# Spreading eight gate rows over the partitions: four transposes of a repeated column in place of one fp32 product with a diagonal

## The reference, cut to what matters

```python
mod = c_act @ w_ada[l] + b_ada[l]
sh1, sc1, g1, sh2, sc2, g2, sh3, sc3, g3 = jnp.split(mod, N_MOD, axis=-1)
x = x + 0.5 * g1[:, None, :] * swiglu(modulate(x, sh1, sc1), ffn1_gate[l], ffn1_up[l], ffn1_down[l])
x = x + g2[:, None, :] * token_mix(modulate(x, sh2, sc2), ...)
x = x + 0.5 * g3[:, None, :] * swiglu(modulate(x, sh3, sc3), ffn2_gate[l], ffn2_up[l], ffn2_down[l])
# hybrid layer: x + gate1 * (merged @ w_o), then x + gate2 * moe, without the 0.5
```

## Time and profile before

| | |
|---|---|
| Three timed runs | 1815.82, 1820.74, 1822.90 us, median 1820.74 |
| The profiled execution's own time | 1816.8 us |
| Its span, first to last instruction | 1815.0 us |
| PE busy | 1741.0 us, 96% |
| DVE busy | 1379.6 us, 76% |
| ACT busy | 967.7 us, 53% |
| DMA | 437.43 MB, 241 GB/s over the span |
| Mean granted clock of PE | 0.988 |
| L1032, diagonals on DVE | 64 instructions, 281 ns each in the middle of the list |
| L1892, products with diagonals on PE | 32 records, 592 ns each |

### The profile page before, as it was taken

One profiled execution on the slowest core, in us unless ns is written; L12 is line 12 of the kernel. 1 busy time (PEld: TensorE's weight loads), 2 busy tenths in 40 slices (PEclk: granted clock), 3 DMA queues, 4 the chain that ended last, 5 costly groups with the idle time before them and its releaser, 6 DMA issues.

```text
span 1815.0 us, 24952 instructions
## 1 busy us (share of the span) xinstructions
PE 1741.0 (96%) x8621; PEld 1404.7 (77%) x8621; DVE 1379.6 (76%) x2129; ACT 967.7 (53%) x1471; POOL 47.0 (3%) x92
## 2 busy tenths in 40 slices
PE   5999999999999999999989999999899998999998
PEld 3788778787788878887878877887687876888876
DVE  6887776766876678777687578876767578999997
ACT  3544364664644454444546655444536547777775
POOL 0000000000000000000000000000000000000000
PEclk8999999999999999999999999999899999999999
DMA  8988753225576758785623347987373444999994
GB/s 361 353 345 301 288 194 139 73 94 206 209 282 253 260 191 338 299 305 224 232 77 110 113 166 291 345 306 270 143 300 116 186 163 152 375 351 352 367 348 161
DMA packets 61802, 437.43 MB, mean 241 GB/s; under 512 B 6816, under 2 KB 7328, under 8 KB 9504
## 3 DMA queue, kind: packets, MB, share of 16 engines
q1 hardware_dynamic: 47504, 339.27, 49.7%
q0 software_dynamic: 12672, 92.28, 13.6%
q10 hardware_dynamic: 1552, 4.89, 0.7%
HBM read 435.36 MB, written 1.05 MB: 240 GB/s over the span
## 4 chain that ended last, share of the span: by engine, by line
PE 82%; DVE 10%; ACT 5%; issue 2%; DMA 1%; ACTq 0%; DVEq 0%; SPq 0%; POOLq 0%
PE bank L1843 24%; PE bank L1844 24%; PE bank L1845 24%; DVE w_lo L984 3%; PE bank L2087 2%; DVE ada_w L1016 2%; ACT w_hi L516 1%; PE bank L2105 1%; PE bank L1931 1%; DMA ada_w<-ada_pairs 1%; PE bank L2067 1%; DVE arena L1319 1%; PE bank L1892 1%; PE bank L2423 1%; ACT arena L533 1%
## 5 line engine op out<-in xcount | busy, mean ns | idle before, releaser
L984 DVE TENSOR_TENSOR w_lo<-raw,w_hi 128x1024 fp32r<-128x1024 f32 x426 | 501.5, 1220 | 200.8 <-ACT w_hi L516 199.9
L516 ACT ACTIVATE w_hi<-raw 128x1024 fp32r<-128x1024 f32 x426 | 426.5, 1052 | 338.8 <-PE bank L1845 335.5
L1843 PE MATMUL bank<-w_hi,uT_hi 128*128 128x512 f32 (+2 forms) x1408 | 552.9, 393 | 20.3 <-DVE uT_lo L1336 13.1
L1844 PE MATMUL bank<-w_lo,uT_hi 128*128 128x512 f32 (+2 forms) x1408 | 538.8, 383 | 0.0
L1845 PE MATMUL bank<-w_hi,uT_lo 128*128 128x512 f32 (+2 forms) x1408 | 538.3, 382 | 0.0
L1843 PEld LDWEIGHTS bank<-w_hi,uT_hi 128*128 128x128 f32 x1408 | 267.0, 190 | 81.0 <-DVE uT_lo L1336 15.1
L1845 PEld LDWEIGHTS bank<-w_hi,uT_lo 128*128 128x128 f32 x1408 | 266.7, 189 | 52.0
L1844 PEld LDWEIGHTS bank<-w_lo,uT_hi 128*128 128x128 f32 x1408 | 267.3, 190 | 48.1 <-issue 1.2
L1843 PE MATMUL bank<-w_hi,r_arena 128*128 128x512 f32 (+1 forms) x744 | 297.2, 399 | 4.8 <-DVE r_arena L1741 2.3
L1844 PE MATMUL bank<-w_lo,r_arena 128*128 128x512 f32 (+1 forms) x744 | 293.9, 395 | 0.0
L1845 PE MATMUL bank<-w_hi,r_arena 128*128 128x512 f32 (+1 forms) x744 | 291.6, 392 | 0.0
(11 more groups left out here) (339 smaller groups left out, 1476.5 us busy)
## 6 DMA issues: line engine op xcount, KB each, us to landing
raw<-weight_stream SPq DMA_DIRECT2D x216, 1024.0 KB, 4.9
ada_w<-ada_pairs POOLq DMA_DIRECT2D x88, 1024.0 KB, 5.3
raw<-expert_blocks SPq DMA_DIRECT2D x48, 1024.0 KB, 4.8
ada_w<-expert_blocks SPq DMA_DIRECT2D x32, 1024.0 KB, 4.9
cmpw<-expert_blocks SPq DMA_DIRECT2D x16, 1024.0 KB, 4.9
arena<-ada_pairs SPq DMA_DIRECT2D x5, 1024.0 KB, 13.1
ada_w<-ada_pairs SPq DMA_DIRECT2D x3, 1024.0 KB, 13.5
cmpw<-compress_w ACTq DMA_DIRECT2D x2, 1024.0 KB, 7.9
```

The lines of the kernel that those rows point to most:

```text
L516: act.activation(w_hi[:, b], v, ACT.Copy).then_inc(hi_done, 1)
L984: V.tensor_tensor(w_lo[:, b], v, f32(w_hi[:, b]), ALU.subtract).then_inc(split_done, 1)
L1843: pe.matmul(dst, xh, w_hi[:, off:off + n], start=first, stop=False, skip_group_check=True)
L1844: pe.matmul(dst, xh, w_lo[:, off:off + n], start=False, stop=False, skip_group_check=True)
```

## The change

The eight columns are turned one by one. A column of `modf`, read with step zero, is a 128x128 matrix in which every column is the same; transposed, each of its rows is the column, laid out along the row. So four 128x128 transposes with the identity give the same 512 values on all partitions that the product of ones with four diagonals gave.

- DVE keeps the addition of the bias. The eight multiplications with the identity go. In stages 0, 2, 3 and 5 one small multiplication of the eight columns by 0.5 comes instead. In the other four nothing comes, and the wait for the addition goes too.
- PE has four transposes with a 128x128 output for each of the 16 products. They stand where the product stood, and the last one signals.
- The columns of even and odd stages have places of their own (`modf` grows from 24 to 32 columns). DVE waits for the products of the stage two before, ahead of writing.
- Nothing else moves, and no transfer changes.

```diff
-        xn, uTf, diag = at(0, T, D), at(2048, KD, S), at(4096, KD, P)
-        diag_mix, diag_hyb = at(5120, KD, P), at(3072, KD, P)
+        xn, uTf = at(0, T, D), at(2048, KD, S)
...
+        def gate_column(n, k):
+            return modf[:, 16 + 8 * (n % 2) + k:17 + 8 * (n % 2) + k]
...
-            def gate(n, src, half=1.0, diag=diag):
-
-                link(V.tensor_tensor(modf[:, 16:24], src, vec[:, bass.ds(V_BADA + n * 24 + 16, 8)], ALU.add))
-                for k in range(KD):
-                    d = V.tensor_scalar(diag[:, k], ident, modf[:, 16 + k:17 + k], half, ALU.mult, ALU.mult)
-                d.then_inc(diag_done, 1)
+            def gate(n, src, half=1.0):
+
+                g = modf[:, 16 + 8 * (n % 2):24 + 8 * (n % 2)]
+                if n >= 2:
+                    dve.wait_ge(gate_psum, 2 * n - 2)
+                e = V.tensor_tensor(g, src, vec[:, bass.ds(V_BADA + n * 24 + 16, 8)], ALU.add)
+                if half != 1.0:
+                    link(e)
+                    e = V.tensor_scalar(g, g, half, None, ALU.mult)
+                e.then_inc(gate_known, 1)
...
-            def gate(n, h, b, diag=diag):
-                pe.wait_ge(diag_done, n + 1)
-                pe.matmul(b[:, :], ones, diag[:, 4 * h:4 * h + 4], start=True, stop=True, skip_group_check=True).then_inc(gate_psum, 1)
+            def gate(n, h, b):
+                pe.wait_ge(gate_known, n + 1)
+                for i in range(4):
+                    m = pe.transpose(b[:, i * P:(i + 1) * P], gate_column(n, 4 * h + i).to_broadcast([P, P]), ident)
+                m.then_inc(gate_psum, 1)
```

More of the change, by code:

```diff
@@ L119, in program @@
         lvec = sb("lvec", [P, L_ALL])
-        modf = sb("modf", [P, 24])
+        modf = sb("modf", [P, 32])
         stat = sb("stat", [P, 112])
@@ L279, in program @@
         hL_psum, hL_hi_done, hL_ready = sem("hL_psum"), sem("hL_hi_done"), sem("hL_ready")
-        diag_done, gate_psum, gate_ready = sem("diag_done"), sem("gate_psum"), sem("gate_ready")
+        gate_known, gate_psum, gate_ready = sem("gate_known"), sem("gate_psum"), sem("gate_ready")
         uT_psum, uTf_done_a, uTf_done_v = sem("uT_psum"), sem("uTf_done_a"), sem("uTf_done_v")
@@ L1161, in ffn1 @@
                 modulation(stage + 1, mods[:, 0:16])
-                gate(stage + 1, mods[:, 16:24], diag=diag_mix)
+                gate(stage + 1, mods[:, 16:24])
                 for j in (20, 21):
@@ L1553, in _ @@
                 if m == 1:
-                    gate(n6, mods[:, 56:64], diag=diag_hyb)
+                    gate(n6, mods[:, 56:64])
                 if m == 2:
@@ L2137, in _ @@
                 for h, b in enumerate((HT, GU[1])):
-                    gate(l * 3 + 1, h, b, diag_mix)
+                    gate(l * 3 + 1, h, b)
                 for m in range(2):
@@ L2304, in _ @@
                 if m == 2:
-                    gate(n6, 0, HT, diag_hyb)
+                    gate(n6, 0, HT)
                 if m == 3:
                     pe.wait_ge(gate_ready, 2 * n6 + 1)
-                    gate(n6, 1, HT, diag_hyb)
+                    gate(n6, 1, HT)
             seen = {m: set() for m in (4, 5, 6)}
```

## The result

Five timed runs of the changed kernel gave 1802.56 to 1803.80 us, median 1803.52. Five of before beside them gave a median of 1820.74. The medians lie 17 us apart. The ratio of the runs is 0.9918, 95% interval 0.9902 to 0.9933, which is 15 us, 12 to 18. Both are more than twice the 6.6 of the forecast. The profiled executions compare as 1815.0 to 1801.7 us of span, 13.3 less.

A forecast was written before the change was run, and what follows sets the result against it. PE was taken to bound the kernel, with 82% of the span's chain of waits. Gains of 2.5, 0.8 and 3.3 us sum to 6.6, taking 1818.8 us to 1812.2 us; range 1806 to 1820, chance 0.58.

The forecast's parts named there:

- the price of an exchange: Where PE is dense, four transposes at 0.44 us replace a product of 0.86 us, giving 0.42 us each.
- dear turn: Rival: step-zero loads make four transposes cost 0.90 us, as much as the product; 1815.7 us in all, chance 0.14.
- serial turns: Rival: on PE, each load and transpose runs one after the other, 1.64 us for four; 1827 us, chance 0.05.
- stages 0 and 3: First products gain 0.42 us each on PE; at the hidden-tile wait, diagonals removed from DVE gain 1.67 us each.
- DVE's part: Last unit of stages 0 and 3: without diagonals DVE delivers the hidden tile 1.67 us earlier, 3.3 us for both.
- stages 1, 4 and 7 gain nothing: Products after a normalisation only fill PE's wait for uT_lo, so exchanging them gains 0.
- the clock rival: After normalisations in stages 1, 4 and 7 PE's clock falls, costing 1.57 us each, 4.7 in all; 1816.9 us, chance 0.14.
- The gates' sum: All gains at the gates together: 2.5 us in stages 2, 5, 6, and 0.8 plus 3.3 us at stages 0, 3; 6.6 us.
- 2.5 + 0.8 + 3.3 = 6.6 us: Whole forecast gain: six dense products, first products of stages 0 and 3, and DVE's diagonals of stages 1 and 4.
- gains in stages without a gate: Sign named in advance that would show the forecast wrong; no size was given.
- its diagonals are swallowed by DVE's wait for a row of conditioning weights: Stage 5: DVE runs on into a 1.52 us wait, which takes up all the time saved; no gain counted.

The follow-up runs named there:

- e2: The changed kernel with odd stages' gate columns in a tensor of their own, so every other tensor keeps its old address; ratio to before 0.9949.
- e11: The changed kernel with each group of four turns made twice over in stages 0, 2, 3, 5 and 6; ratio to before 0.9929.
- e8: The changed kernel with DVE still building the eight diagonals of stages 1 and 4, read by nobody; ratio to before 0.9952.
- e10: The changed kernel with each group of four turns made twice over in stages 1, 4 and 7; ratio to before 0.9917.
- e1: The kernel before with only modf widened from 24 to 32 columns, moving every later tensor by 32 bytes; ratio to before 0.9958.
- e3: The kernel before with gaps of 32 bytes ahead of and behind r_arena, putting it at a multiple of 64 bytes; ratio to before 0.9942.
- e16: The changed kernel with one gap of 64 bytes ahead of r_arena; median 1800.00 us, ratio to before 0.9916.
- e4: The changed kernel with two gaps of 32 bytes, so cst, modf, cmpw, r_arena and arena begin at multiples of 64 bytes; 1798.70 us, ratio to before 0.9896.
- e5: The kernel before with r_arena alone moved by 96 bytes, to a multiple of 128; ratio to before 0.9935.

## Why the prediction was wrong

**Right: the price of an exchange.** It is 0.42 us by the forecast, and 0.42 to 0.48 by the steps in the traces of e2 and after. With a dear turn or serial turns the starts at 207.08 and 207.51 would lie 0.9 or 1.6 us apart, and they lie 0.43 apart. Turns come every 0.11 us, and four more in a row add 0.44 (e11). The Trainium skill (TensorE: Matmul & The Clock Gate, section LDWEIGHTS, loading the stationary operand) makes a load of 128 columns 0.107 us. The distance between turns agrees with that, with step zero too; the record of one load is longer, 0.137 us.

**Right: stages 0 and 3.** DVE's part is 1.67 by forecast; each stage gained 2.1 in e2 (0.42, then 0.42 and 1.27 at the tile), where the forecast has 0.42 + 1.67. e8 shows that the diagonals are its cause. What the forecast left out is the clock. It read from rows 6 that a wait of 1.73 us behind dense passes leaves the clock at 2.4 GHz. In the trace of before it does, but at 10 of 22 such places it didn't, so a gain of about 1.4 us (the estimate above) has no term.

**Right: stages 1, 4 and 7 gain nothing.** The 1.72 us that the chain puts on the products only covered a wait. e10 shows it with the turns doubled. The clock didn't fall there: 24 transposes and 0.95 us of wait left the granted clock at 1.00 three times. The sentence of the Trainium skill on transposes (TensorE: Matmul & The Clock Gate, Part 4: PE-mode transpose), by which the clock rival would have come, is not borne out for such a stretch.

**The gates' sum was right.** It is 6.6 by the forecast and 6.9 by the steps in e2, whose ratio of 0.9949 is 9 us, 6 to 13 by its interval. One number of the rivals doesn't follow from its own terms: with only the 3.3 us of DVE left the time would be 1815.5 and not 1815.7. Nothing hangs on it.

**Wrong, the step that failed: the sum, "2.5 + 0.8 + 3.3 = 6.6 us", which has gates in it alone and puts the addresses at nothing.** The change also makes `modf` 32 bytes wider. I read that as a place for odd stages, wrote that nothing else moves, and gave it no term. It moved `r_arena` from a distance of 160 to one of 192 modulo 256 from the weights. That shortened some 2160 passes by 4 to 5 ns, 9 us in the trace, 8 us in e1's ratio and 10 in e3's, more than the gates. The forecast says itself what would prove it wrong: gains in stages without a gate. They came. The missing rows were in the profile of before: passes with `r_arena` took 397 ns where the same pass with `uT_hi` took 393, with no instruction between them to explain it.

**Stage 5, a wait that I left out.** The forecast's claim is that its diagonals are swallowed by DVE's wait for a row of conditioning weights. PE waits there too, before (first row), and not after. What differs is the transfer: it landed 7.8 us after its issue before and 5.3 after (second row). The third row is e1, with the diagonals, where it took 7.7 and PE waits again. The next two are e2, without them, where it took 6.6. The last two are e10 and e16, also without them, where it took 7.9 to 8.0:

```profile
1132.80 0.66 PE L1931 MATMUL bank<-cst,arena 128*128 128x128 f32 x4 [1.08 <-DVE arena L1069]
```

```profile
1115.02 1.23 DVE L1018 CUSTOM_DVE_ANT_0 ada_w<-ada_w,cmpw 128x1024 f32<-128x1024 f32 x1 [0.56 <-DMA ada_w<-ada_pairs]
```

```profile
1129.36 0.66 PE L1931 MATMUL bank<-cst,arena 128*128 128x128 f32 x4 [1.22 <-DVE arena L1069]
```

```profile
1114.68 1.23 DVE L1019 CUSTOM_DVE_ANT_0 ada_w<-ada_w,cmpw 128x1024 f32<-128x1024 f32 x1 [1.80 <-DMA ada_w<-ada_pairs]
1122.34 0.66 PE L1940 MATMUL bank<-cst,arena 128*128 128x128 f32 x4
```

```profile
1124.42 0.66 PE L1939 MATMUL bank<-cst,arena 128*128 128x128 f32 x4 [1.49 <-DVE arena L1075]
```

```profile
1122.59 0.66 PE L1940 MATMUL bank<-cst,arena 128*128 128x128 f32 x4 [1.57 <-DVE arena L1076]
```

e3 has the diagonals, a landing of 5.5, and no such wait of either engine. e4 has no diagonals, a landing of 6.6, and 0.26 us on PE. So PE waits where the transfer lands late, with the diagonals or without them, and 1.2 us of the traces' difference is a transfer's landing and not the gates. Why it differs from execution to execution wasn't tried.

## What to carry to other kernels

## What the runs showed of the hardware

- The pitch of dense 128x512 fp32r passes depends on the distance between stationary and moving operand in SBUF: 227 to 229 ns at a multiple of 256 bytes, 232 to 234 at distances of 32, 64, 128, 160 and 224, 229 at 192. Other distances, other shapes and other types weren't tried, and the cause within the chip isn't settled.
- The fastest kernel is the change with `r_arena` at a multiple of 256 from `w_hi`: e4 1798.70 us, ratio 0.9896 to before. That is 19 us, of which e5 gives 12 without the exchange.
- A stationary operand read with step zero along its columns loads in 137 ns (an ordinary one in 141), and a transpose with it follows every 0.11 us, as with an ordinary one.
- 16 transposes, eight more and a wait of 0.95 us left the granted clock at 1.00 at three places of three.
- Waits of 1.49 to 2.11 us at the end of stages 0 and 3 were followed by a granted clock of 0.50 at 10 of 22 places, waits of up to 0.47 us at none of 14. What decides between the 10 and the 12 isn't known.
